# Two DRAM accumulators in turn for the routed experts' results, with no wait behind each scatter

## The chip, the cores and the metric

The kernel runs on one core of a Trainium2 chip. The metric is the device time of one execution in microseconds (us), the median of several runs. A core has a matrix engine (PE, with a separate row PEld for its weight loads), a vector engine (DVE), a scalar engine (ACT), GpSimd (POOL), a queueing engine (SP) and 16 DMA engines that all its queues share.

## What is computed

One layer of a decoder for 512 prompt tokens and 64 sample tokens (576 in all, width 1024, all float32): a mixer of pooling and two kinds of attention, then a mixture of experts. Only the last matters here:

```python
scores = jax.nn.sigmoid(jnp.einsum('nd,de->ne', xf, w_router, ...))
_, top_idx = lax.top_k(scores + router_bias.astype(jnp.float32), TOP_K)      # 8 of 64 experts
top_w = top_s / jnp.sum(top_s, axis=-1, keepdims=True) * ROUTED_SCALE
...
def one_block(args):
    xb, e = args
    return swiglu(xb, we_gate[e], we_up[e], we_down[e])                      # 1024 -> 256 -> 1024
y_rows = lax.map(one_block, (x_rows, block_exp)).reshape(n_rows, d)
return jax.ops.segment_sum(y_rows * row_w[:, None], row_tok, num_segments=n_tok + 1)[:n_tok]
...
y = routed_experts(...) + swiglu(xf, ws_gate, ws_up, ws_down)                # plus a shared expert
```

Tokens are sorted by expert into blocks of 128 rows that belong to one expert each; a block's rows are gathered, go through the expert, and are added back to their tokens. After it come an RMSNorm, a gate and the residual sum.

## The kernel before

Each engine runs a program of its own, written out by hand, and they meet in semaphores. The routed part is a loop over pairs of blocks (35 pairs with these inputs; the number is computed on the chip). In a pair, j is 0 or 1.

- **POOL** (lines 985 to 1017) gathers the rows of the next pair from the DRAM tensor `h2rows` into `xg[:, j]` (L1001), as soon as `t_done` says that PE has transposed the rows of this pair. Then it copies the pair's row numbers and weights into `scol` and `wcol` (L1006, L1007; `cols_ready`). Then, for each j, it waits until ACT and DVE have written the result `yb[:, j]`, issues a scatter that adds it to the DRAM tensor `yacc` (L1014, an indirect DMA with an add), **waits for its landing** (L1015) and counts `added`. All of POOL's DMAs are in queue q0.
- **PE** transposes the gathered rows (L2275, 8 instructions for a block), multiplies with gate and up of block 0 and of block 1 (16 records of L1836 each at 0.43 us), turns the activations (L2290) and multiplies with down. The transposes of block 1 wait for the pair before to be copied out of its bank.
- **ACT and DVE** copy the transposed rows (L1271, L1799), form the activation (L1294, L1804), copy it back turned (L1281), and write `yb` (L1288, L1809), scaled by `wcol`, after `added` says that the scatter before has read the buffer. ACT also waits for the weights and passes that on to PE as `weights_in` (L1264).
- **SP** (L845, L847, L851) fetches each expert's gate, up and down (1 MB each, queue q1) into one of two buffers. Gate and up of an expert are issued when PE has finished gate and up of the expert two before it (`gu_done`), down when the down product has (`d_done`), strictly one after another: the second block's gate and up stand behind the first block's down.

Before the loop the shared expert's results go into `yacc` (L857), which also has 128 rows for padding (L858). After it SP waits for all scatters, reads `yacc` back (L881), ACT takes the sum of squares (L1312), DVE normalises (L1817 to L1827) and SP writes the outputs.

Of the kernel before, what the change touches and what calls it, by code (L numbers as in the profile page):

```python
# [47 lines left out]
def parts(t):  # L48
    return P if t < PT_ else NS
# [258 lines left out]
def build(nc, x_prompt, x_sample, cache_b1, cache_b2, cache_b3, cache_c, state_pool, c_prompt, c_sample,  # L308
# [14 lines left out]
    with ExitStack() as ctx:  # L323
# [8 lines left out]
        def at(off, *dims):  # L332
# [4 lines left out]
            if len(dims) == 3:  # L337
# [34 lines left out]
        h2rows = nc.dram_tensor("h2rows", [TOK, D], F32, kind="Internal").ap()  # L372
        yacc = nc.dram_tensor("yacc", [TOK + P, D], F32, kind="Internal").ap()

# [104 lines left out]

        g2mod = at(8 * D, 2, D)  # L480


# [39 lines left out]
                             "at_ready", "d_done", "y_act", "y_dve"))  # L522
        added, weights_in = sem("added"), sem("weights_in")
        yacc_in, cols_ready, g2_in = sem("yacc_in"), sem("cols_ready"), sem("g2_in")
        f_in = [sem(f"f_in{t}") for t in range(TILES)]
        f_ssq, f_root, f_rn, f_out = (sem(n) for n in ("f_ssq", "f_root", "f_rn", "f_out"))

# [94 lines left out]
        def _(sp):  # L622
# [232 lines left out]
            for t in range(TILES):  # L855
                wait_emptied(sp, ("sy", t, 1))
                sp.dma_start(yacc[toks(t), :], ysh[0:parts(t), t, :]).then_inc(yacc_in, 16)  # L857
            sp.dma_start(yacc[TOK:TOK + P, :], ysh[:, 0, :]).then_inc(yacc_in, 16)  # L858

# [18 lines left out]
            for j in range(2):  # L878
                sp.wait_ge(y_out[j], 16 * n_pairs)
            for t in range(TILES):  # L880
                sp.dma_start(ysh[0:parts(t), t, :], yacc[toks(t), :]).then_inc(f_in[t], 16)  # L881
            for j in range(2):
# [13 lines left out]
        def _(pool):  # L896
# [86 lines left out]
            n_pairs = pool.value_load(pairs[0:1, 0:1], min_val=1, max_val=NBLK // 2)  # L983
            pool.sem_inc(added, 2)

            for j in range(2):
# [4 lines left out]
                                        ).then_inc(xg_in[j], 16)  # L991
            pool.wait_ge(yacc_in, 16 * (TILES + 1))
            with pool.Fori(0, n_pairs) as i:

                for j in range(2):

                    pool.wait_ge(t_done, 2 * i + j + 3)
                    pool.tensor_copy(icol[:, j:j + 1], rowtok[:, bass.ds(2 * i + j + 2, 1)]).then_inc(icol_ready, 1)  # L998
                    pool.wait_ge(icol_ready, 2 * i + j + 3)
                    pool.sem_inc(gather_ticks, 1)  # L1000
                    pool.indirect_dma_start(xg[:, j, :], None, h2rows,  # L1001
                                            bass.IndirectOffsetOnAxis(ap=icol[:, j:j + 1], axis=0)
                                            ).then_inc(xg_in[j], 16)

                for j in range(2):
                    pool.tensor_copy(scol[:, j:j + 1], addrow[:, bass.ds(2 * i + j, 1)]).then_inc(cols_ready, 1)  # L1006
                    pool.tensor_copy(wcol[:, j:j + 1], wtab[:, bass.ds(2 * i + j, 1)]).then_inc(cols_ready, 1)  # L1007
                pool.wait_ge(cols_ready, 4 * i + 4)

                for j in range(2):  # L1010
                    pool.wait_ge(y_act, 2 * i + j + 2)
                    pool.wait_ge(y_dve, 2 * i + j + 2)
                    pool.sem_inc(gather_ticks, 1)
                    pool.indirect_dma_start(yacc, bass.IndirectOffsetOnAxis(ap=scol[:, j:j + 1], axis=0),  # L1014
                                            yb[:, j, :], None, compute_op=ALU.add).then_inc(y_out[j], 16)  # L1015
                    pool.wait_ge(y_out[j], 16 * i + 16)
                    pool.sem_inc(added, 1)


        @block.scalar  # L1020
        def _(act):
# [245 lines left out]
            with act.Fori(0, n_pairs) as i:  # L1267
# [15 lines left out]
                def result(j):  # L1283

                    act.wait_ge(added, 2 * i + j + 1)
                    act.wait_ge(d_done, 2 * i + j + 3)
                    act.wait_ge(cols_ready, 4 * i + 2 * j + 2)
                    act.activation(yb[:, j, 0:512], psb[6 if j == 0 else 2][:, :], ACT.Copy,  # L1288
                                   scale=wcol[:, j:j + 1]).then_inc(y_act, 1)
# [16 lines left out]
            for t in range(TILES + 1):  # L1306
                if t < TILES:
                    r = parts(t)
                    act.wait_ge(f_in[t], 16)
                    if t:  # L1310
                        act.wait_ge(f_ssq, t)
                    act.activation(junk2[0:r, :], ysh[0:r, t, :], ACT.Square,  # L1312
                                   accum_out=stat[0:r, 3, t:t + 1]).then_inc(f_ssq, 1)
# [7 lines left out]
        def _(dve):  # L1321
# [371 lines left out]
            shared_act(1)  # L1693

            total, nblk, ends, r0 = (starts[:, n, :] for n in range(4))

# [99 lines left out]
            with dve.Fori(0, n_pairs) as i:  # L1796
# [8 lines left out]
                for j in range(2):  # L1805
                    dve.wait_ge(added, 2 * i + j + 1)
                    dve.wait_ge(d_done, 2 * i + j + 3)
# [3 lines left out]


            for t in range(TILES + 1):
                if t < TILES:
                    st = stat[0:parts(t), 3, t:t + 1]
                    dve.wait_ge(f_ssq, t + 1)
                    dve.tensor_scalar(st, st, 1.0 / D, EPS, ALU.mult, ALU.add).then_inc(f_root, 1)  # L1817
# [521 lines left out]
```

## Time and profile before

| | |
|---|---|
| median of 3 runs | 2154.64 us (2152.85 to 2161.73) |
| span of the profiled execution | 2140.2 us |
| its mean granted TensorE clock | 0.915 |
| busy in it: PE / PEld / DVE / ACT / POOL | 1869.5 / 1155.5 / 463.4 / 369.2 / 298.4 us |
| loop over pairs in it | 1098.6 to 2105.1 us |
| weights fetched by SP's queue q1 in the loop | 62 experts of 3 MB |

Times in a trace are counted from the span's start. A wait is shown as the idle time of an engine in front of an instruction, and the arrow names what ended it. The landing of a DMA is the time at which its semaphore tells of it. The clock is the share of full speed that the chip granted to TensorE.

### The profile page before, as it was taken

To read this page: it belongs to the slowest core of one execution; us is meant where nothing else is said; L and a number is where in the kernel's file an instruction comes from. 1 tells how busy PE (TensorE), PEld (TensorE's weight loads), DVE (VectorE), ACT (ScalarE), POOL (GpSimd) and SP (SyncE) were. 2 spreads that over 40 slices of the span, in tenths; PEclk is the share of its full clock that TensorE was granted. 3 is DMA by queue.
4 is the path that set the end of the run, shared out by engine and by line. 5 is a ranking of instruction groups with operands and counts; after the bars stand their busy time and mean duration, and the time that the engine had idled before them with its cause. 6 is when DMAs were issued, how large, how long until landed. Compare 5 with 4: busy or idle time off the path is not lost.

```text
span 2140.2 us, 22425 instructions
## 1 busy us (share of the span) xinstructions
PE 1869.5 (87%) x6907; PEld 1155.5 (54%) x6908; DVE 463.4 (22%) x1188; ACT 369.2 (17%) x1013; POOL 298.4 (14%) x462
## 2 busy tenths in 40 slices
PE   7899999998899999996968988899789877898873
PEld 1268887878797777544434434444344443344431
DVE  2120001464421111244621111111011111111112
ACT  2100002463320000132101111111111111111111
POOL 0110410020000000010012212222212222211221
PEclk9999999589999999998979998999899898998987
DMA  9843693505786543300058888887788788878875
GB/s 308 303 135 37 183 330 129 166 3 187 234 257 198 157 135 115 121 30 15 30 214 293 261 291 282 285 281 231 265 289 265 253 255 303 284 255 289 285 239 152
DMA packets 147723, 446.40 MB, mean 209 GB/s; under 512 B 10734, under 2 KB 76142, under 8 KB 121879
## 3 DMA queue, kind: packets, MB, share of 16 engines
q1 hardware_dynamic: 125555, 326.43, 44.0%
q0 software_dynamic: 22112, 119.21, 20.7%
q8 instruction: 37, 0.61, 0.1%
q14 instruction: 19, 0.16, 0.0%
HBM read 392.87 MB, written 97.48 MB: 229 GB/s over the span
## 4 chain that ended last, share of the span: by engine, by line
PE 60%; DMA 27%; DVE 5%; issue 4%; SPq 1%; POOL 1%; ACT 1%; POOLq 0%; DVEq 0%; ACTq 0%
PE bank L1836 55%; DMA yacc<-arena,scol 17%; DMA arena<-h2rows,icol 8%; PE bank L2275 2%; PE bank L2058 1%; PE bank L1993 1%; POOL arena L1001 1%; DMA pscale<-in_pool_scale 1%; DMA mods<-arena 1%; DVE arena L1809 1%; DMA arena<-in_w_ada 1%; SPq L639 0%; PE bank L2290 0%; PE bank L1860 0%; POOL icol L998 0%
## 5 line engine op out<-in xcount | busy, mean ns | idle before, releaser
L1836 PE MATMUL bank<-arena 128*128 (+8 forms) x5656 | 1706.2, 459 | 54.1 <-ACTq L1264 15.2
L1836 PEld LDWEIGHTS bank<-arena 128*128 128x128 f32 (+3 forms) x5656 | 987.7, 200 | 675.6 <-issue 564.6
L2275 PE MATMUL bank<-ident,arena 128*128 128x128 f32 x560 | 101.4, 339 | 147.1 <-DMA arena<-h2rows,icol 144.3
L1014 POOL DMA_INDIRECT yacc<-arena,scol x70 | 112.1, 1602 | 505.5 <-DMA yacc<-arena,scol 354.3
L2275 PEld LDWEIGHTS bank<-ident,arena 128*128 128x128 f32 x560 | 86.1, 203 | 178.0 <-DMA arena<-h2rows,icol 115.0
L1033 ACT ACTIVATE arena<-bank 128x512 f32<-128x512 f32 (+7 forms) x152 | 75.9, 505 | 378.7 <-PE bank L1836 223.2
L1804 DVE TENSOR_TENSOR arena<-bank,arena 128x256 f32<-128x256 f32 x70 | 29.7, 425 | 501.5 <-ACT arena L1294 501.5
L1809 DVE TENSOR_SCALAR arena<-bank,wcol 128x512 f32<-128x512 f32 x70 | 51.5, 749 | 223.7 <-POOL wcol L1007 113.9
L1333 DVE COPY arena<-bank 128x512 f32<-128x512 f32 (+8 forms) x74 | 43.7, 593 | 243.1 <-PE bank L1836 178.5
L1294 ACT ACTIVATE arena<-bank 128x256 f32<-128x256 f32 x70 | 26.9, 384 | 372.1 <-PE bank L1836 262.1
L1799 DVE COPY arena<-bank 128x512 f32<-128x512 f32 x70 | 48.4, 692 | 165.6 <-PE bank L2275 165.6
L1288 ACT ACTIVATE arena<-bank,wcol 128x512 f32<-128x512 f32 x70 | 48.1, 687 | 182.1 <-POOL wcol L1007 90.1
L1001 POOL DMA_INDIRECT arena<-h2rows,icol x70 | 70.9, 1013 | 59.8 <-POOL icol L998 56.6
L1271 ACT ACTIVATE arena<-bank 128x512 f32<-128x512 f32 x70 | 41.8, 597 | 176.9 <-PE bank L2275 175.9
L970 POOL DMA_DIRECT2D out<-in_cache_b x24 | 12.1, 513 | 346.4 <-PE bank L1836 280.1
L1180 ACT ACTIVATE arena<-bank 128x288 f32<-128x288 f32 x48 | 19.7, 411 | 217.1 <-PE bank L1836 217.1
L1281 ACT ACTIVATE arena<-bank 128x256 f32<-128x256 f32 x70 | 26.9, 384 | 160.7 <-PE bank L2290 160.7
L998 POOL COPY icol<-arena 128x1 uint32 x70 | 13.2, 189 | 240.9 <-DMA yacc<-arena,scol 229.2
L2290 PEld LDWEIGHTS bank<-ident,arena 128*128 128x128 f32 x140 | 27.3, 195 | 33.1 <-issue 24.7
L1618 DVE SCALAR_TENSOR_TENSOR arena<-bank,pscale,arena 128x288 f32<-128x288 f32 x16 | 8.3, 518 | 169.0 <-PE bank L1836 169.0
L978 POOL TENSOR_TENSOR arena<-arena 128x1024 f32<-128x1024 f32 (+1 forms) x5 | 11.7, 2341 | 169.7 <-DVE arena L1674 169.7
L1123 ACT ACTIVATE arena<-arena,nmx 128x128 f32<-128x128 f32 (+1 forms) x80 | 34.8, 437 | 1.2 <-DVE nmx L1504 1.2
(249 smaller groups left out, 690.8 us busy)
## 6 DMA issues: line engine op xcount, KB each, us to landing
arena<-in_we_gate SPq DMA_DIRECT2D x64, 1024.0 KB, 6.4
arena<-in_we_up SPq DMA_DIRECT2D x64, 1024.0 KB, 10.3
arena<-in_we_down SPq DMA_DIRECT2D x64, 1024.0 KB, 7.9
out<-in_cache_b POOLq DMA_DIRECT2D x8, 4080.0 KB, 16.1
arena<-in_w_ada SPq DMA_DIRECT2D x12, 2048.0 KB, 17.6
arena<-in_cache_b SPq DMA_DIRECT2D x18, 1024.0 KB, 7.6
arena<-in_w_in SPq DMA_DIRECT2D x7, 2048.0 KB, 8.2
arena<-in_w_in SPq DMA_DIRECT2D x24, 512.0 KB, 5.8
```

Of the source, the lines that this page charges most:

```text
L1001: pool.indirect_dma_start(xg[:, j, :], None, h2rows, bass.IndirectOffsetOnAxis(ap=icol[:, j:j + 1], axis=0)).then_inc(xg_in[j], 16)
L1014: pool.indirect_dma_start(yacc, bass.IndirectOffsetOnAxis(ap=scol[:, j:j + 1], axis=0), yb[:, j, :], None, compute_op=ALU.add).then_inc(y_ ...
L1033: act.activation(out, pick(bank), ACT.Copy).then_inc(emptied["A"], 1)
L1123: ins = act.activation(v, v, ACT.Exp, bias=nmx[:, s % 4, h:h + 1], accum_out=den[:, s % 4, h:h + 1])
L1271: act.activation(xT[:, j, 0:512], psb[2 * j][:, :], ACT.Copy).then_inc(xt_act, 1)
L1288: act.activation(yb[:, j, 0:512], psb[6 if j == 0 else 2][:, :], ACT.Copy, scale=wcol[:, j:j + 1]).then_inc(y_act, 1)
L1333: dve.tensor_copy(out, pick(bank)).then_inc(emptied["D"], 1)
L1799: dve.tensor_copy(xT[:, j, 512:1024], psb[2 * j + 1][:, :]).then_inc(xt_dve, 1)
L1804: dve.tensor_tensor(a, psb[4 + j][:, FF:2 * FF], e, ALU.mult).then_inc(a_ready, 1)
L1809: dve.tensor_scalar(yb[:, j, 512:1024], psb[7 if j == 0 else 3][:, :], wcol[:, j:j + 1], None, ALU.mult).then_inc(y_dve, 1)
L1836: return pe.matmul(out, lhsT, rhs, start=first, stop=last)
L2275: ins = pe.transpose(psb[2 * j + k // 4][:, P * (k % 4):P * (k % 4 + 1)], xg[:, j, k:D:KD], ident[:, :])
```

## The change

There are two accumulators, `yacc[0]` and `yacc[1]`; block j of every pair adds to `yacc[j]`. POOL no longer waits behind a scatter. The wait for the landing of the scatter of the same j moves to the next pair, in front of the copies of `scol`, whose buffer the scatter reads. ACT and DVE wait for `y_out[j]` itself, and the count `added` is gone. `yacc[1]` begins as zeros (a memset of `yb[:, 1]` on DVE, stored by SP tile by tile), the padding rows are stored by POOL, and at the end both accumulators are read and DVE sums them.

```diff
-        yacc = nc.dram_tensor("yacc", [TOK + P, D], F32, kind="Internal").ap()
+        yacc = [nc.dram_tensor(f"yacc{j}", [TOK + P, D], F32, kind="Internal").ap() for j in range(2)]
...
+        yother = at(A_W1, TILES, D)
...
-                sp.dma_start(yacc[toks(t), :], ysh[0:parts(t), t, :]).then_inc(yacc_in, 16)
-            sp.dma_start(yacc[TOK:TOK + P, :], ysh[:, 0, :]).then_inc(yacc_in, 16)
+                sp.dma_start(yacc[0][toks(t), :], ysh[0:parts(t), t, :]).then_inc(yacc_in, 16)
+                if t == 0:
+                    sp.wait_ge(zeros_ready, 1)
+                sp.dma_start(yacc[1][toks(t), :], yb[0:parts(t), 1, :]).then_inc(yacc_in, 16)
...
-                sp.wait_ge(y_out[j], 16 * n_pairs)
+                sp.wait_ge(y_out[j], 16 * n_pairs + 16)
             for t in range(TILES):
-                sp.dma_start(ysh[0:parts(t), t, :], yacc[toks(t), :]).then_inc(f_in[t], 16)
+                sp.dma_start(ysh[0:parts(t), t, :], yacc[0][toks(t), :]).then_inc(f_in[t], 16)
+                sp.dma_start(yother[0:parts(t), t, :], yacc[1][toks(t), :]).then_inc(f_in[t], 16)
...
-            pool.sem_inc(added, 2)
...
-            pool.wait_ge(yacc_in, 16 * (TILES + 1))
+            pool.wait_ge(zeros_ready, 1)
+            for j in range(2):
+                pool.dma_start(yacc[j][TOK:TOK + P, :], yb[:, 1, :]).then_inc(y_out[j], 16)
+            pool.wait_ge(yacc_in, 16 * 2 * TILES)
...
                 for j in range(2):
+
+                    pool.wait_ge(y_out[j], 16 * i + 16)
                     pool.tensor_copy(scol[:, j:j + 1], addrow[:, bass.ds(2 * i + j, 1)]).then_inc(cols_ready, 1)
...
-                    pool.indirect_dma_start(yacc, bass.IndirectOffsetOnAxis(ap=scol[:, j:j + 1], axis=0),
+                    pool.indirect_dma_start(yacc[j], bass.IndirectOffsetOnAxis(ap=scol[:, j:j + 1], axis=0),
                                             yb[:, j, :], None, compute_op=ALU.add).then_inc(y_out[j], 16)
-                    pool.wait_ge(y_out[j], 16 * i + 16)
-                    pool.sem_inc(added, 1)
...
-                    act.wait_ge(added, 2 * i + j + 1)
+                    act.wait_ge(y_out[j], 16 * i + 16)
...
-                    act.wait_ge(f_in[t], 16)
+                    act.wait_ge(f_sum, t + 1)
...
+            dve.wait_ge(h2_out, 16 * PT_)
+            dve.memset(yb[:, 1, :], 0.0).then_inc(zeros_ready, 1)
...
-                    dve.wait_ge(added, 2 * i + j + 1)
+                    dve.wait_ge(y_out[j], 16 * i + 16)
...
+            def both(t):
+
+                r = parts(t)
+                dve.wait_ge(f_in[t], 32)
+                dve.tensor_tensor(ysh[0:r, t, :], ysh[0:r, t, :], yother[0:r, t, :], ALU.add).then_inc(f_sum, 1)
+
+            both(0)
             for t in range(TILES + 1):
+                if t + 1 < TILES:
+                    both(t + 1)
```

POOL's loop over pairs before, in the order in which it is issued. The two scatters are L1014; the second waits for `y_out0`, the landing of the first, and the loop's end waits for `y_out1`.

```order
104 L998 ISA [waits t_done]
105 L998 COPY icol<-arena 128x1
106 L1001 DMA arena<-h2rows,icol 128x1024 [waits icol_ready]
...
120 L1011 REGISTER_ALU [waits cols_ready]
121 L1014 DMA yacc<-arena,scol 704x1024 [waits y_act,y_dve]
122 L1016 ISA
123 L1014 DMA yacc<-arena,scol 704x1024 [waits y_out0,y_act,y_dve]
124 L993 REGISTER_ALU [waits y_out1]
125 L993 COMPARE_AND_BRANCH
```

The same loop after the change.

```order
106 L1004 ISA [waits t_done]
107 L1004 COPY icol<-arena 128x1
108 L1007 DMA arena<-h2rows,icol 128x1024 [waits icol_ready]
...
114 L1014 ISA [waits y_out0]
115 L1014 COPY scol<-arena 128x1
...
118 L1014 ISA [waits y_out1]
119 L1014 COPY scol<-arena 128x1
...
124 L1022 DMA yacc<-arena,scol 704x1024 [waits y_act,y_dve] x2
125 L999 REGISTER_ALU
```

The waits for landings have moved from behind each scatter to a place behind the next pair's gathers, so neither the second scatter nor the gathers stand behind a landing.

DVE's tail before: from the first tile's statistics to the end of its sum with the residual and on to the second tile's statistics.

```order
791 L1817 TENSOR_SCALAR stat<-stat 128x1 [waits f_ssq] x2
792 L1823 RECIPROCAL stat<-stat 128x1 [waits f_rn]
793 L1826 SCALAR_TENSOR_TENSOR arena<-arena,stat 128x1024 [waits g2_in,dve_step]
794 L1827 TENSOR_TENSOR arena<-arena 128x1024 [waits dve_step]
795 L1817 TENSOR_SCALAR stat<-stat 128x1 [waits f_ssq]
```

The same place after the change, where L1826 is the sum of the two accumulators.

```order
793 L1826 TENSOR_TENSOR arena<-arena 128x1024 [waits f_in0]
794 L1826 TENSOR_TENSOR arena<-arena 128x1024 [waits f_in1]
795 L1835 TENSOR_SCALAR stat<-stat 128x1 [waits f_ssq]
796 L1826 TENSOR_TENSOR arena<-arena 128x1024 [waits f_in2]
797 L1835 TENSOR_SCALAR stat<-stat 128x1 [waits f_ssq]
798 L1841 RECIPROCAL stat<-stat 128x1 [waits f_rn]
799 L1844 SCALAR_TENSOR_TENSOR arena<-arena,stat 128x1024 [waits g2_in,dve_step]
800 L1845 TENSOR_TENSOR arena<-arena 128x1024 [waits dve_step]
```

A sum of 1024 columns stands in front of each tile's work, one tile ahead.

## Rows read from the trace of the kernel before

**Rows 1.** The page, part 4: the chain that ended last, by line.

```profile
PE bank L1836 55%; DMA yacc<-arena,scol 17%; DMA arena<-h2rows,icol 8%; PE bank L2275 2%; PE bank L2058 1%; PE bank L1993 1%; POOL arena L1001 1%; DMA pscale<-in_pool_scale 1%; DMA mods<-arena 1%; DVE arena L1809 1%; DMA arena<-in_w_ada 1%; SPq L639 0%; PE bank L2290 0%; PE bank L1860 0%; POOL icol L998 0%
```

**Rows 2.** Waits in the loop (1130 to 2110): total us, times, longest us.

```profile
POOL yacc L1014 <- DMA yacc<-arena,scol: 354.3, 34, 12.3
...
POOL icol L998 <- DMA yacc<-arena,scol: 229.2, 34, 10.4
...
PE bank L2275 <- DMA arena<-h2rows,icol: 129.5, 34, 8.4
...
DVE arena L1809 <- POOL wcol L1007: 113.9, 16, 9.2
...
PE bank L1836 <- ACTq L1264: 15.2, 12, 2.4
```

**Rows 3.** Timeline of POOL: start, us, instruction, [idle time before it and what ended it].

```profile
1549.84 1.62 POOL L1014 DMA_INDIRECT yacc<-arena,scol  x1 [7.65 <-DVE arena L1809]
1561.96 1.57 POOL L1014 DMA_INDIRECT yacc<-arena,scol  x1 [10.51 <-DMA yacc<-arena,scol]
1572.37 0.18 POOL L998 COPY icol<-arena 128x1 uint32 x1 [8.84 <-DMA yacc<-arena,scol]
1573.39 1.03 POOL L1001 DMA_INDIRECT arena<-h2rows,icol  x1 [0.83 <-POOL icol L998]
```

**Rows 4.** Timeline of PE over the same pairs and the next two.

```profile
1553.53 7.03 PE L1836 MATMUL bank<-arena 128*128 x16
1561.56 3.70 PE L1836 MATMUL bank<-arena 128*128 x8 [1.00 <-ACTq L1264]
...
1581.58 1.97 PE L2275 MATMUL bank<-ident,arena 128*128 128x128 f32 x8 [5.57 <-DMA arena<-h2rows,icol]
...
1609.91 1.05 PE L2275 MATMUL bank<-ident,arena 128*128 128x128 f32 x8
...
1633.15 1.04 PE L2275 MATMUL bank<-ident,arena 128*128 128x128 f32 x8
```

**Rows 5.** Timeline of SP's queue: down of one block, gate of the next.

```profile
1548.10 0.33 SPq L851 DMA_DIRECT2D arena<-in_we_down  x1
1550.19 0.33 SPq L845 DMA_DIRECT2D arena<-in_we_gate  x1
```

**Rows 6.** Stretches: engines' busy us (instructions), granted clock, DMA share, GB/s.

```profile
1098.60:2105.10 1006.50, 855.83 (x2372) 423.85 (x2372) 129.14 (x210) 143.68 (x280) 213.48 (x349) 0.92 0.83 269
1549.00:1566.00 17.00, 15.83 (x50) 7.90 (x49) 2.56 (x5) 2.65 (x5) 3.19 (x2) 1.00 1.00 349
1900.00:2000.00 100.00, 80.36 (x226) 40.63 (x225) 13.10 (x21) 14.20 (x27) 18.90 (x31) 0.88 0.88 293
```

**Rows 7.** DMA queues, 1106 to 2106: packets, MB, share of 16 engines' time.

```profile
q1 hardware_dynamic: 26826, 195.26, 52.3%
q0 software_dynamic: 19837, 72.22, 30.2%
```

**Rows 8.** DMA queues, 1555 to 1561, one scatter beside weights.

```profile
q1 hardware_dynamic: 204, 1.42, 59.2%
q0 software_dynamic: 144, 0.52, 44.0%
```

**Rows 9.** Before the loop: DVE's timeline, and SP's queue q1 from 1010 to 1084.

```profile
1013.18 0.22 DVE L1698 COPY arena<-bank 128x64 f32<-128x64 f32 x1 [8.11 <-PE bank L1836]
...
q1 hardware_dynamic: 800, 2.88, 10.8%
```

**Rows 10.** Timeline of the tail, POOL, SP, ACT and DVE.

```profile
2109.42 1.58 POOL L1014 DMA_INDIRECT yacc<-arena,scol  x1 [5.33 <-DMA yacc<-arena,scol]
2115.78 2.29 SPq L881 DMA_DIRECT2D arena<-yacc  x5
2119.39 1.06 ACT L1312 ACTIVATE arena<-arena 128x1024 f32<-128x1024 f32 x1 [14.39 <-DMA arena<-yacc]
...
2135.63 1.22 DVE L1827 TENSOR_TENSOR arena<-arena 64x1024 f32<-64x1024 f32 x1
```

More of the change, by code:

```diff
@@ L522, in build @@
                              "at_ready", "d_done", "y_act", "y_dve"))
-        added, weights_in = sem("added"), sem("weights_in")
+        weights_in, zeros_ready = sem("weights_in"), sem("zeros_ready")
         yacc_in, cols_ready, g2_in = sem("yacc_in"), sem("cols_ready"), sem("g2_in")
         f_in = [sem(f"f_in{t}") for t in range(TILES)]
-        f_ssq, f_root, f_rn, f_out = (sem(n) for n in ("f_ssq", "f_root", "f_rn", "f_out"))
+        f_sum, f_ssq, f_root, f_rn, f_out = (sem(n) for n in ("f_sum", "f_ssq", "f_root", "f_rn", "f_out"))
         def wait_fill(eng, key):
```

## The prediction, made before the changed kernel was run

> **What bounds the kernel now.** I read the chain first, then the waits of the loop, then timelines of single pairs. In the chain [rows 1] PE's matmuls hold 55%, and behind them stand two transfers: scatters 17%, gathers 8%. The loop over 35 pairs takes 1006.5 of the 2140.2 us [rows 6], 28.76 us a pair, and this is where the change acts. Its waits [rows 2] show one chain from end to end: POOL's second scatter waits for the first to land (354.3 us, 34 times), POOL's next gather waits for the second (229.2 us), PE's transposes wait for that gather (129.5 us), and DVE's results wait for the weights column that POOL copies late (113.9 us, 16 times). One pass through it: first scatter 1549.84, second 1561.96, next pair's gather 1573.39 [rows 3], transposes 1581.58, after 5.57 us of idle [rows 4]. Nothing but POOL's order made that gather late, since its buffer was free once PE had done the transposes before gate and up at 1553.53 [rows 4].
>
> What the pair costs without that chain shows in one pair that waited for nothing: from transposes 1609.91 to transposes 1633.15 [rows 4], **23.24 us**. So 35 x (28.76 - 23.24) = 193 us of the loop are idle time or slow clock. The stalls also cost clock: the transposes after a stall take 1.97 us for 8, the unstalled ones 1.05 and 1.04 [rows 4], which is 1.2 against 2.4 GHz; the loop's mean clock is 0.92 [rows 6]. The Trainium skill, "TensorE: Matmul & The Clock Gate", part 1, says that a gate passes half of the clock's pulses when the engine has been idle; the trace agrees, by the 1.97 and 1.04 us.
>
> **The change, part by part.**
>
> *The wait behind each scatter goes.* POOL's program for a pair then is: gathers, wait for both scatters of the pair before, four small copies, two scatters. The gathers can be issued as soon as the transposes are done, some 20 us ahead of their use instead of 8 us. PE's 129.5 us of waits for gathers and DVE's 113.9 us for the column should nearly vanish, and with them the clock's falls. If nothing took their place, the loop would be 35 x 23.24 = 813 us, 193 less.
>
> *What is late next: the DMA engines.* In 1000 us of the loop the weights' queue q1 takes 52.3% and POOL's queue q0 30.2% of the engines' time [rows 7]: 523 and 302 us. 1000 us hold 34.8 pairs, so q0 costs 302 / 34.8 = 8.7 us a pair (two gathers, two scatters). The loop fetches 62 experts, 523 / 62 = 8.44 us each, 16.9 us in a pair that fetches two. Together **25.6 us of DMA time for a full pair**, more than PE's 23.24. By SP's issues 28 pairs fetch two experts, 6 fetch one, the last none; those 7 are left to PE (8.44 + 8.7 is under 23.24). The stretch 1549 to 1566 has a DMA share of 1.00 while PE is busy 15.83 of 17 us [rows 6], so a full DMA is possible, but only while enough is queued. SP does not queue ahead: the second block's gate and up are issued 2.09 us after the first block's down (1548.10, 1550.19) [rows 5], and PE wants them at 1553.53 + 7.03 = 1560.56. It got them at 1561.56, with one scatter beside them: 1.00 us late [rows 4]. Over the loop such waits were 15.2 us, the longest 2.4 [rows 2]. This 1.00 us I add to every full pair, since all of them will now run on this tight schedule: 26.6 us.
>
> Sum of the loop: 28 x 26.6 + 7 x 23.24 = 744.8 + 162.7 = 907.5 us, **99.0 us less** than 1006.5.
>
> Bounds of this term: at the low end transfers fit in, and a full pair costs PE's time and the 1.00 us seen: 28 x 24.24 + 162.7 = 841.4, 165 less. At the high end DMA reaches only the share of a dense 100 us of before, 0.88 [rows 6]: 25.6 / 0.88 = 29.1, 28 x 29.1 + 162.7 = 977.5, 29 less. I take the value between, nearer to the trace's 1.00 over 17 us than to 0.88, because that 0.88 has POOL's own order in it, which emptied q0 for 8 us at a time.
>
> *Waits that move.* The copies of the columns now wait for both landings. One scatter by itself kept POOL waiting 12.3 us at the longest [rows 2], 14 with its issue. Its first 5 us bring no data: all 0.52 MB of the one issued at 1549.84 [rows 3] moved between 1555 and 1561 [rows 8]. Two in a row share that start, so with q0's 8.7 us doubled by sharing both are in after at most 5 + 17 = 22 us; as the gathers behind them are in the 8.7 too, and a scatter took 6 us of its time, more likely 5 + 12 = 17. They are issued just before and just after the transposes, and the column is wanted 23.24 less two result steps of some 2 us, that is 19 us after them. That is thin; it mostly costs nothing, and a late pair pays 1 or 2 us, which the high end holds. ACT's and DVE's waits on y_out ask for the same landing as the column does, so they add nothing.
>
> *Before the loop.* DVE's memset stands in front of a wait of 8.11 us for PE [rows 9]; even at 1.22 us, the price of 1024 columns in a sum [rows 10], it is hidden. Without that cover it would cost 1.22. SP's five extra stores lie in a stretch where q1 is busy 10.8% of 74 us, 8.0 us for 2.88 MB [rows 9]; hidden too. POOL's two padding stores, 1.05 MB or 2.9 us at that rate, now lie behind the first gathers, beside the first weights; one such store was in SP's queue before. Bounds 0 and 2.9; I take **1.5 us**, half, since only part of the first weights is awaited.
>
> *After the loop.* The second scatter is issued after the last result instead of at 2109.42 [rows 10], about 3.5 us earlier, but the DMA time of the first is in its way: 3 us gained. Then twice the bytes are read back. The first tile came 3.6 us after SP's issue at 2115.78 [rows 10]; its partner adds 1.3 us, and one sum of 1.22 us [rows 10] precedes its square. After that DVE is the bound, with five sums more, 6.1 us in all. The first one's wait and four further sums, less what DVE idled between tiles: 7 us. Bounds 5 and 9. Net **4 us** lost.
>
> Sum: -99.0 + 1.5 + 4 = -93.5. The profiled span becomes 2140.2 - 93.5 = 2046.7. The runs' median lies 14.4 us above that span (launch and end lie outside it), and I shift it alike: 2154.6 - 93.5 = **2061 us**.
>
> **The rivals.**
>
> *A. The weights' wait takes the gather's place, and the clock falls again: slower.* Place: PE in front of the second block's gate and up. From 1555 to 1561 one scatter took 44.0% and the weights 59.2% of the engines' time [rows 8], so each us in which q0 is busy there costs the weights 0.4 us. Before, the scatter's data began to move only near 1555, so the weights had 1550 to 1555 alone. If the first scatter moves earlier, at 2.5 us, and the second and a gather follow without a gap, weights are beside q0 for the whole of 1552 to 1564 and finish 3 us later still: a wait of 4 us. If such a wait halves the clock, as the 5.57 us idle did, gate and up of a block (7.03 us) take up to twice as long, say 3.5 us more. A full pair is then 23.24 + 4 + 3.5 = 30.7, the loop 28 x 30.7 + 162.7 = 1022, the time 2154.6 + 16 + 5.5 = **2176**. It decides at (1006.5 - 162.7) / 28 = 30.1 us a full pair. Against it: the 12 waits of that kind seen were 1.3 us on average [rows 2] and PE's clock stayed at 1.00 in that stretch [rows 6]. The Trainium skill, "DMA: Bandwidth & Descriptors", section "Queues, rings and completion order", says that a DMA engine goes round the queues that have work, packet by packet, so a full q0 always takes its turns from the weights; the trace agrees with 44.0 against 59.2%. By this rule alone, with no order between the transfers, this rival is what the change invites.
>
> *B. The gathers are late again, in q0.* They now stand behind two scatters in one queue. If q0's 8.7 us are doubled by sharing (17.4) plus 5 us of start, the second gather lands some 22 us after the transposes, wanted after 24 to 25. For it: little room. If it came 2 us late in every full pair, with DMA empty meanwhile, the pair is 28.6 and the loop 963.5, 43 less: **2117**.
>
> *C. All fits.* Low end of the loop: 2154.6 - 165 + 5.5 = **1995**. For it: weights can come 1.00 us late and no later. Against: 25.6 us of DMA do not fit in 24.24, unless packets got slow only by contention.
>
> *D. The change doesn't do what it says:* POOL would still wait for landings, now in front of the columns, and results wait for the columns. If that cost what it did before (113.9 us, twice as often since now in every pair), 228 us against the 243 that go: about **2145**. Against: the landings have a whole pair's time.
>
> **How the numbers follow.** Forecast 2035 to 2090: 0.55. C and what lies towards it, under 2035: 0.20. B and poor DMA use, 2090 to 2144: 0.13. D, within 0.5% (10.8 us, about what a measurement of this kernel tells from no change): 0.05. A: 0.07. The range leaves out A, D, the worst of B and the best of C: 2005 to 2125. Faster 0.88, same 0.05, slower 0.07.
>
> **What the profile after would show.** Right, if POOL's waits for scatters shrink to a few us, gathers are issued within 3 us of the transposes, the time between the unawaited transposes is 25.5 to 27.5 us in full pairs, the DMA share in the loop rises from 0.83 to 0.91, the clock to about 1.0, and the wait of L1836 for L1264 grows from 15.2 us to 60 or 90. Wrong, if PE's waits for weights exceed 3 us a pair and the clock stays at 0.92 (A), if transposes still wait for gathers (B), or if DVE's results wait for the column in most pairs (D). The tail should read: last result to end 39 us instead of 35.

## The result, and the profile after

| | before | after |
|---|---|---|
| median of 4 runs | 2154.80 us (2152.85 to 2161.73) | 2013.76 us (2002.48 to 2022.74) |
| ratio to before | | 0.9339, 95% interval 0.9302 to 0.9376 |
| span of the profiled execution | 2140.2 us | 2010.7 us |
| loop over pairs in it | 1006.5 us | 872.6 us |
| last result to the end | 35.1 us | 40.4 us |
| mean granted clock in it | 0.915 | 0.946 |

The changed kernel is 141 us faster. The range held it, the size did not: 2061 us had been forecast. The span shrank by 129.5 us: the loop gave 133.9, the part before it 0.9, and the tail cost 5.3. The medians moved 11.5 us further than the spans. The profiled execution of after was itself timed, at 2012.53 us, so only 1.8 us lie around its span; with the same 1.8 us the profiled execution of before took some 2142 us, a quick one beside its median of 2154.8. The prediction had put all of its 14.4 us around the span.

After, the page's part 4, the chain that ended last, by line, which answers to [rows 1] (L1854 is the helper that was L1836, L1022 the scatter, L1007 the gather):

```profile
PE bank L1854 66%; DMA arena<-in_we_up 14%; PE bank L2076 1%; PE bank L2011 1%; PE bank L2293 1%; DMA pscale<-in_pool_scale 1%; PE bank L2308 1%; DMA arena<-h2rows,icol 1%; DMA arena<-in_w_ada 1%; DMA mods<-arena 1%; SPq L871 1%; SPq L870 1%; SPq L846 1%; SPq L640 0%; DMA yacc<-arena,scol 0%
```

Scatters have gone from 17% to nothing and gathers from 8 to 1%. In their place stands a transfer that was not in the chain before: the weights of the up product, 14%. The waits in the loop (1130 to 1975) answer to [rows 2]:

```profile
POOL yacc L1022 <- DVE arena L1818: 352.3, 66, 13.2
POOL scol L1014 <- DMA yacc<-arena,scol: 217.2, 62, 4.8
DVE arena L1818 <- PE bank L1854: 192.6, 68, 3.0
...
PE bank L1854 <- ACTq L1270: 42.5, 25, 5.1
```

POOL now waits for results, as it should. It still waits 217.2 us for landings, in front of the columns, but nobody stands behind it: DVE's results (L1818) wait for PE alone, and no wait for gathers is left in this stretch. PE's wait for weights, passed on by ACT at L1270, has grown from 15.2 us in 12 times to 42.5 in 25.

One full pair on PE after, beside [rows 4], and the loop and a stretch of it beside [rows 6]:

```profile
1745.14 1.05 PE L2293 MATMUL bank<-ident,arena 128*128 128x128 f32 x8
...
1747.33 7.03 PE L1854 MATMUL bank<-arena 128*128 x16
1755.14 3.70 PE L1854 MATMUL bank<-arena 128*128 x8 [0.78 <-ACTq L1270]
...
1769.43 1.05 PE L2293 MATMUL bank<-ident,arena 128*128 128x128 f32 x8
```

```profile
1097.70:1970.30 872.60, 820.85 (x2372) 400.74 (x2372) 129.80 (x210) 143.53 (x280) 216.22 (x349) 0.99 0.91 311
...
1300.00:1400.00 100.00, 95.16 (x279) 46.46 (x278) 15.51 (x25) 17.01 (x33) 26.40 (x42) 1.00 0.97 327
```

The pair takes 24.29 us, the 23.24 of an unstalled one and 1.05 more, mostly the 0.78 us for weights. It is one of the shorter ones: of the 25 waits for weights half are over 1.33 us. The clock is at 0.99 instead of 0.92 in the loop, and the same 2372 instructions keep PE busy for 820.85 instead of 855.83 us: of the 134 us gained, 35 are the faster clock in PE's own work. The DMA share rose from 0.83 to 0.91. The queues from 1106 to 1960, beside [rows 7]:

```profile
q1 hardware_dynamic: 26886, 195.75, 59.6%
q0 software_dynamic: 19895, 72.41, 32.5%
```

In the tail SP reads both accumulators once both scatters have landed, and ACT's first square waits for DVE's sum, beside [rows 10]:

```profile
1980.20 0.33 SPq L884 DMA_DIRECT2D arena<-yacc  x1
...
1986.25 1.06 ACT L1318 ACTIVATE arena<-arena 128x1024 f32<-128x1024 f32 x1 [16.00 <-DVE arena L1826]
```

### The profile page after: what moved, and what is told of

Same layout as the page of the kernel before. It is cut to its first block, busy times and chain, and to the rows that moved or that the text cites. A ratio compares the mean times of both kernels' runs of the same rounds, so it can differ in the third digit from the quotient of the medians.

```text
span 2010.7 us, 22441 instructions
## 1 busy us (share of the span) xinstructions
PE 1832.8 (91%) x6907; PEld 1131.9 (56%) x6908; DVE 470.2 (23%) x1194; ACT 368.4 (18%) x1013; POOL 302.3 (15%) x464
## 4 chain that ended last, share of the span: by engine, by line
PE 71%; DMA 18%; DVE 4%; SPq 4%; issue 2%; ACT 1%; POOL 0%; ACTq 0%; POOLq 0%; DVEq 0%
PE bank L1854 66%; DMA arena<-in_we_up 14%; PE bank L2076 1%; PE bank L2011 1%; PE bank L2293 1%; DMA pscale<-in_pool_scale 1%; PE bank L2308 1%; DMA arena<-h2rows,icol 1%; DMA arena<-in_w_ada 1%; DMA mods<-arena 1%; SPq L871 1%; SPq L870 1%; SPq L846 1%; SPq L640 0%; DMA yacc<-arena,scol 0%
## 5 line engine op out<-in xcount | busy, mean ns | idle before, releaser
L1854 PE MATMUL bank<-arena 128*128 (+8 forms) x5656 | 1695.0, 457 | 82.6 <-ACTq L1270 42.5
L1854 PEld LDWEIGHTS bank<-arena 128*128 128x128 f32 (+3 forms) x5656 | 979.6, 198 | 699.8 <-issue 586.4
L1022 POOL DMA_INDIRECT yacc<-arena,scol x70 | 112.1, 1602 | 373.7 <-DVE arena L1818 368.7
L1818 DVE TENSOR_SCALAR arena<-bank,wcol 128x512 f32<-128x512 f32 x70 | 52.6, 751 | 198.3 <-PE bank L1854 198.3
L2293 PE MATMUL bank<-ident,arena 128*128 128x128 f32 x560 | 78.0, 283 | 21.0 <-DMA arena<-h2rows,icol 15.4
L2293 PEld LDWEIGHTS bank<-ident,arena 128*128 128x128 f32 x560 | 71.5, 193 | 43.5 <-issue 19.5
L1007 POOL DMA_INDIRECT arena<-h2rows,icol x70 | 70.7, 1010 | 60.2 <-POOL icol L1004 56.7
L1014 POOL COPY scol<-arena 128x1 uint32 x70 | 12.9, 184 | 220.2 <-DMA yacc<-arena,scol 217.2
L2308 PEld LDWEIGHTS bank<-ident,arena 128*128 128x128 f32 x140 | 27.4, 195 | 33.1 <-issue 24.7
```

The lines of the kernel that those rows point to most:

```text
L1007: pool.indirect_dma_start(xg[:, j, :], None, h2rows, bass.IndirectOffsetOnAxis(ap=icol[:, j:j + 1], axis=0)).then_inc(xg_in[j], 16)
L1022: pool.indirect_dma_start(yacc[j], bass.IndirectOffsetOnAxis(ap=scol[:, j:j + 1], axis=0), yb[:, j, :], None, compute_op=ALU.add).then_inc ...
L1818: dve.tensor_scalar(yb[:, j, 512:1024], psb[7 if j == 0 else 3][:, :], wcol[:, j:j + 1], None, ALU.mult).then_inc(y_dve, 1)
L1854: return pe.matmul(out, lhsT, rhs, start=first, stop=last)
L2293: ins = pe.transpose(psb[2 * j + k // 4][:, P * (k % 4):P * (k % 4 + 1)], xg[:, j, k:D:KD], ident[:, :])
L2308: ins = pe.transpose(psb[j][:, k * P:(k + 1) * P], act3[:, 3 * j + 2, k:FF:2], ident[:, :])
```

## The experiments

Each kernel ran in turns with the kernel before on the same chip. Ratios are to the kernel before; pairs are timed from ACT's copy of one pair's second block to that of the next, and numbered from 0. A full pair is one in which SP fetches two experts. A trace is of one run of its kernel, which can lie up to 18 us from the median (e4's does), so loop lengths that differ by a few us are not told apart.

### Which of the two waits matters

e1 puts both waits back behind the scatters, in the kernel with two accumulators:

```diff
                     pool.indirect_dma_start(yacc[j], ...).then_inc(y_out[j], 16)
+                    pool.wait_ge(y_out[j], 16 * i + 32)
```

> The changed kernel with the wait for the landing put back behind each scatter; the two accumulators, the stores ahead of the loop and the sums behind it stay. If the gain is all in POOL's order (my theory), the loop is back at some 1000 us and the whole at 2155 to 2165, the time before plus some 5 us of tail. If the second accumulator itself helped (the rival: two adds to one tensor slow each other in memory), it stays under 2120.

Measured: 2161.9 us, ratio 1.002 (0.9987 to 1.0052). The time is in the range of its theory. The loop is back at 1024 us, and the three waits of [rows 2] are back too:

```profile
POOL yacc L1022 <- DMA yacc<-arena,scol: 273.0, 26, 12.5
...
POOL icol L1004 <- DMA yacc<-arena,scol: 195.5, 28, 10.4
...
PE bank L2294 <- DMA arena<-h2rows,icol: 119.3, 28, 8.4
```

(waits of e1, 1130 to 1960, a shorter stretch than in [rows 2]). The second accumulator by itself gives nothing. All of the gain is POOL's order, which the second accumulator allows: with it the two scatters of a pair never add to the same tensor.

e2 puts a wait behind the first scatter only, e3 behind the second only:

```diff
+                    if j == 0:                # e3: j == 1
+                        pool.wait_ge(y_out[j], 16 * i + 32)
```

> The changed kernel with a wait for the landing behind the first scatter only: the second scatter, and the gathers behind it, start some 8 us later than in the changed kernel, but no gather waits for the second landing. Theory: most of the gain comes from freeing the gathers of the second landing, since gathers issued 11 to 13 us after the transposes still have about 12 us; 2015 to 2050. Rival: the two scatters must overlap for any gain, over 2080.

> The changed kernel with a wait for the landing behind the second scatter only: the scatters overlap, but the next gathers are issued only when the second has landed, some 15 us after the transposes instead of 3. Theory: gathers then land about when PE wants them or a few us later, 2040 to 2100. Rival: the place of the wait does not matter, only that there is one less, and e2 and e3 give the same time within 10 us.

Measured: e2 2038.1 us, ratio 0.944 (0.9375 to 0.9504), loop 892 us; e3 2079.5 us, ratio 0.9645 (0.958 to 0.971), loop 932 us. Both fell in their theories' ranges. Taking away the second wait alone (e2) brings some 119 of the 141 us; taking away the first alone (e3) some 77. They sum to more than the whole: either one removed shortens the same chain. But e3's range was met for another reason than the one given. Its gathers, issued some 17 us after the transposes begin (4.5 us in the changed kernel), land 5.3 us later in the median, and PE waits only 9.1 us for them in all. What it loses shows in the weights, which are later, and with them in the clock (72 us of the loop at half speed, against 20 in the changed kernel). Why later gathers go with later weights is not shown:

```profile
POOL icol L1004 <- DMA yacc<-arena,scol: 357.7, 31, 13.3
...
PE bank L1856 <- ACTq L1272: 63.5, 23, 5.4
...
PE bank L2295 <- DMA arena<-h2rows,icol: 9.1, 6, 2.5
```

(waits of e3, 1130 to 1960).

### One accumulator with the changed order

If the second accumulator gives nothing, one should do, as in e2: the second scatter waits for the landing of the first, since both may add to the same row (what would be lost without that wait was not run), and the next gathers follow its issue. The padding rows are stored in two halves, so that both landing counts start as in the changed kernel.

```diff
-                    pool.indirect_dma_start(yacc[j], ...).then_inc(y_out[j], 16)
+                    pool.indirect_dma_start(yacc, ...).then_inc(y_out[j], 16)
+                    if j == 0:
+                        pool.wait_ge(y_out[j], 16 * i + 32)
...
-                dve.tensor_tensor(ysh[0:r, t, :], ysh[0:r, t, :], yother[0:r, t, :], ALU.add).then_inc(f_sum, 1)
```

> One accumulator as before, but with the changed order: the second scatter waits for the landing of the first, and the next gathers are issued behind it with no wait for its own landing (that comes in front of the next columns). No second tensor, no sums at the end. By e2 the loop takes some 892 us; the tail is 5 us shorter than with two accumulators: 2028 to 2040. If two adds to one tensor cost the loop anything by themselves it is over 2045.

Measured: 2025.8 us, ratio 0.9366 (0.9326 to 0.9406), the loop 893.0 us and the tail 35.1. That is 2 us under its range of 2028 to 2040, and not over the 2045 of the other theory. The loop is 20 us longer than with two accumulators, as in e2 (892), and the tail 5.3 shorter. By the intervals it can't be told from the changed kernel. Two adds to one tensor cost nothing of their own here when the second waits for the first; two in flight at once on one tensor were not run.

### Does a longer wait for weights bring the clock down?

e5 holds every second expert's gate and up back, to test rival A:

```diff
-                    sp.wait_ge(gu_done, done)
+                    sp.wait_ge(t_done if j == 1 else gu_done, done + 2 if j == 1 else done)
```

> The changed kernel with the gate and up fetch of every second expert held back until PE has transposed the block two after the expert's last: some 2.5 us later than in the changed kernel in a pair whose second block it belongs to, more in the others. It tests rival A, that a longer wait for weights lets the clock fall and costs far more than itself. If waits of 3 to 4 us leave the clock up, a full pair costs 26 to 27.5 us, the whole 2060 to 2110, and the mean clock stays above 0.93. If the clock falls as after the 5.57 us stalls of before, a pair costs 29 us or more, the whole is over 2140 and the half-speed time in the loop is over 100 us (20 in the changed kernel).

Measured: 2335.9 us, ratio 1.0829 (1.0788 to 1.087). This is the side on which the clock falls (over 2140 us, over 100 us at half speed), but far beyond it, because I had the delay wrong. SP's loop runs over experts and PE's over blocks. An expert with two blocks shifts one against the other, and in the shifted pairs PE stands still for about 12 us and not 2.5: these pairs take 35 to 39 us. PE in such a pair:

```profile
1309.16 1.12 PE L2293 MATMUL bank<-ident,arena 128*128 128x128 f32 x8 [0.16 <-ACT arena L1294]
1322.58 12.78 PE L1854 MATMUL bank<-arena 128*128 x24 [12.29 <-issue]
```

Without a stall 24 such records take 10.46 us (e4 and e10, below), so 2.3 us were lost to the clock after the wait; 341 us of the loop were at half speed, most of them while PE stood still. In the pairs that were not shifted (1 and 2) the fetch was held some 2.5 us, and they took 29.3 and 30.3 us instead of 24.8 and 24.6:

```profile
1138.59 5.39 PE L1854 MATMUL bank<-arena 128*128 x8 [4.13 <-ACTq L1270]
...
1167.83 6.49 PE L1854 MATMUL bank<-arena 128*128 x8 [4.05 <-ACTq L1270]
```

So rival A's mechanism exists: a wait of 4 us, as the prediction priced it, and then 1.7 and 2.8 us of clock (8 such records take 3.70 us at full clock), where the prediction had 3.5. Held by 2.5 us, a pair pays about twice the delay; where PE stood for 12 us it paid 13 to 14, little more than the wait itself.

### SP's order

PE's wait for weights, 0.68 us and more a pair, could be SP's lateness or the DMA engines' limit. e4 issues gate and up of both experts of a pass first, then down of both:

```diff
+                both_of = []
...
-                    expert_weights(j, bass.ds(expert, 1), done)
+                    both_of.append((j, bass.ds(expert, 1), done))
+                for args in both_of:
+                    gate_up_weights(*args)
+                for args in both_of:
+                    down_weights(*args)
```

> The changed kernel with SP's order changed: gate and up of both blocks of a pair first, then down of both, so that the second block's gate and up are issued when PE has finished with them, some 3 to 5 us earlier, instead of behind the first block's down. Theory 1 (the wait of about 1 us a pair is SP's order): the wait goes, the loop falls from 873 towards 35 x 23.24 = 813 plus some us, the whole to 1965 to 1985. Theory 2 (the DMA engines are full, 24.3 us of transfers in a pair): the DMA time is the floor, and the whole stays at 2000 to 2015.

Measured: 2046.7 us, ratio 0.9478 (0.9409 to 0.9546), **slower** than the changed kernel, which neither theory had. Pair by pair it falls in two groups. Pairs 1, 2, 19 and 20, in which a pass of SP matches a pair of PE, take 23.2 us with two fetches; here pair 2, 1148.86 to 1172.10:

```profile
1148.86 1.05 PE L2302 MATMUL bank<-ident,arena 128*128 128x128 f32 x8
...
1172.10 1.05 PE L2302 MATMUL bank<-ident,arena 128*128 128x128 f32 x8
```

The shifted pairs take 24 to 30 us, since a block's down now stands behind gate and up of a block that PE finishes half a pair later. A new wait shows there, for down (waits of e4, 1130 to 1960; it was 17.0 us in 7 times in the changed kernel, 1130 to 1975):

```profile
ACT arena L1296 <- DMA arena<-in_we_down: 73.5, 15, 5.7
```

e6 keeps the order and only loads the registers of both experts of a pass ahead:

```diff
+                both_of = []
                 for j in range(2):
                     expert = sp.value_load(...)
                     done = sp.value_load(...)
-                    expert_weights(j, bass.ds(expert, 1), done)
+                    both_of.append((j, bass.ds(expert, 1), done))
+                for args in both_of:
+                    expert_weights(*args)
```

> The changed kernel, in which SP loads the registers of both experts of its loop pass (their numbers and waits) ahead of the first fetch, so that the second's gate and up follow the first's down at once instead of 2.1 us later; the order and the waits are unchanged. If SP's lateness is what PE's wait of about 1 us a pair consists of (theory 1, after e4's pairs of 23.2 us with two fetches), most of these waits go: a loop of 835 to 850 us, the whole 1975 to 1992. If the DMA engines are the floor, nothing moves: 2005 to 2020.

Measured: 2078.3 us, ratio 0.9624 (0.9597 to 0.9652), again slower, and again for the shift. In matching pairs gate follows down after 0.5 us, and they take 23.9 to 24.4 us (24.6 to 25.1 in the changed kernel). In shifted pairs the boundary of SP's pass, now with four register loads, lies between down and gate:

```profile
1217.41 0.33 SPq L852 DMA_DIRECT2D arena<-in_we_down  x1
1220.77 0.34 SPq L846 DMA_DIRECT2D arena<-in_we_gate  x1
```

The gap is 3.36 us instead of 2.09 [rows 5], and PE pays:

```profile
1222.83 7.03 PE L1857 MATMUL bank<-arena 128*128 x16
1233.18 6.69 PE L1857 MATMUL bank<-arena 128*128 x8 [3.32 <-ACTq L1273]
```

A wait of 3.32 us, and then 6.69 us for 8 records that take 3.70 at full clock. **A gap 1.3 us longer made these pairs some 4 us longer** (28.6 us in the median where the changed kernel has 24.8): about 2.5 us of wait and 3 of clock in the pair shown, against 0.8 us of wait. The expectation was missed, but the run shows that a longer gap makes the wait longer. Whether a shorter one takes all of it away it leaves open: in the matching pairs 0.42 to 0.90 us stayed.

e8 therefore turns SP's loop round by one step, so that the next expert's registers are loaded before the wait for the down product, whatever the shift:

```diff
                 for j in range(2):
+                    e, done = fetch_of(2 * i + (j + 2))
+                    following, then = fetch_of(2 * i + (j + 3))
+                    down_weights(j, e, done)
+                    gate_up_weights(1 - j, following, then)
```

> The changed kernel with SP's loop turned round by one step: it loads the registers of the next expert before it waits for the down product, so gate and up follow the down ahead of them at once, in pairs of either alignment. In the kernel where the registers of two experts were loaded together, pairs whose gap grew from 2.1 to 3.4 us took 4 us longer and those whose gap shrank 0.5 us less. If that gap is the cause of the waits for weights, nearly every full pair takes 23.2 to 23.9 us, the loop 820 to 840, the whole 1958 to 1980. If the DMA engines are the floor (24.3 us), it stays over 2000.

Measured: 1991.9 us, ratio 0.9257 (0.9229 to 0.9284), better than the changed kernel. The gap is 0.53 us in all pairs and the bad pairs are gone (waits for weights 23.7 us in 25 times, 1.6 at most). But full pairs take 24.2 to 24.5 us (one 24.8; 23.2 only the four behind a pair with one fetch), not 23.2 to 23.9, and the total lies between the ranges of both theories. The usual wait has stayed. The down product's fetch and PE's start on the second block behind it, first in the changed kernel, then in e8:

```profile
1766.19 0.33 SPq L852 DMA_DIRECT2D arena<-in_we_down  x1
1779.32 3.69 PE L1854 MATMUL bank<-arena 128*128 x8 [0.68 <-ACTq L1270]
```

```profile
1724.58 0.33 SPq L855 DMA_DIRECT2D arena<-in_we_down  x1
1737.68 3.70 PE L1873 MATMUL bank<-arena 128*128 x8 [0.80 <-ACTq L1289]
```

It is 13.1 us in both, though e8's gate was issued 0.53 us behind the down and the other 2.08 (1768.27). Over all pairs the changed kernel's waits for weights run from 0.68 to 5.11 us, half of them over 1.33, and e8's from 0.75 to 1.57, half of them over 0.93. So a long gap at SP makes waits longer, but some 0.8 us is left even with the shortest. What is left is the order, down ahead of gate and up, and the time that the 3 MB then take.

> The kernel with one accumulator, the second scatter behind the landing of the first and the gathers behind its issue, with SP's loop turned round. Its tail is 5 us shorter than with two accumulators, but its second scatter and gathers go some 8 us later. If the weights' lateness was what separated its loop (893 us) from the two accumulators' (873), both come to the same loop and it is 5 us faster: 1953 to 1975. If the late gathers cost it by themselves, its loop stays 15 us or more longer: 1975 to 1995.

Measured: e9 2020.2 us, ratio 0.9398 (0.9369 to 0.9426). The loop is 880.0 us against e8's 848.1: with SP's long gaps gone, one accumulator's later scatters and gathers do cost, some 32 us in the loop for 6 in the tail. Not by gathers that PE waits for (0.8 us, 1130 to 1930), but again by the weights: PE's wait for them is 43.3 us in 24 times. So two accumulators are worth 1.4% here, once the weights are in time. The second theory held in direction; the time lay 25 us over its range.

Last, e10 shifts e4's passes by one expert, so that they match PE's pairs where e4's did not:

```diff
...
+            e, done = fetch_of(2)
+            gate_up_weights(0, e, done)
+            down_weights(0, e, done)
+            with sp.Fori(0, more - 1) as i:
+                e, done = fetch_of(2 * i + 3)
+                following, then = fetch_of(2 * i + 4)
+                gate_up_weights(1, e, done)
+                gate_up_weights(0, following, then)
+                down_weights(1, e, done)
+                down_weights(0, following, then)
...
```

> As e4 (gate and up of two experts first, then down of both), but with the two experts of a pass of SP's loop shifted by one, so that a pass matches PE's pair where e4's did not. In e4 pairs 1, 2, 19 and 20, which fetch two experts and match, took 23.2 us and the 23 others with two fetches 25 to 30. If SP's order in relation to PE's pair is the cause, it is now the other way round: pairs 5 to 10, 14 to 17 and 24 to 33 take 23.2 to 23.6 us, pairs 1, 2, 19 and 20 about 27.5, the loop 830 to 850, the whole 1970 to 1990. If the DMA engines need 24.3 us for two fetches over many pairs in a row, and e4's pairs were only single ones that drew on a pause before, the matching pairs stay at 24.2 us or more and the whole at 1995 or more.

Measured: **1978.7 us**, ratio 0.9198 (0.9153 to 0.9243), the loop 835.8 us. Pairs 5 to 10, 14 to 17 and 24 to 33 all take 23.2 us, and pairs 1 and 2 went from 23.2 in e4 to 29.1 and 28.4 (19 and 20, to 24.9 and 25.9). Two stretches of such pairs, and the queues from 1690 to 1780:

```profile
1690.00:1780.00 90.00, 89.35 (x266) 44.44 (x265) 14.49 (x24) 16.40 (x32) 24.81 (x40) 1.00 1.02 365
1200.00:1350.00 150.00, 148.86 (x447) 74.41 (x446) 25.10 (x40) 27.55 (x53) 41.12 (x64) 1.00 1.02 359
```

```profile
q1 hardware_dynamic: 3454, 25.17, 68.9%
q0 software_dynamic: 2106, 7.67, 33.3%
```

PE is busy 89.35 of 90 us, with a DMA share of 1.02 beside it. (A share is the sum of the packets' times, so it can come out a little over 1.) So the DMA engines are full but not in the way: all transfers of a full pair fit in 23.24 us. This kernel beats the others with these inputs. Its order suits the shift that these inputs happen to have; e8's serves both.

## Why the prediction was right in kind and too small

- **What bounds the kernel.** Right. The chain through both landings to the gather was the loop's stall, as e1 shows by putting it back, and nothing in the changed kernel waits for a gather or a column.
- **The loop, -99.0 us forecast, -133.9 measured.** Here the sum failed, in the term of 26.6 us for a full pair. With 7 pairs at 23.24, 872.6 us leave 25.4 for each of the 28 full ones; 18 of them took 24.2 to 25.2, and a few with longer waits for weights 26 to 31. Two steps made the term too large. First, 25.6 us of DMA time a full pair: in the stretch of e10 above 90 us hold 3.87 full pairs at 68.9 + 33.3%, which is 23.8 us a pair. By the same reckoning the changed kernel's own records give 24.4 us. The records of before charge 8% more than e10's for the same transfers, why is not shown: a packet's time there is no measure of the least it can take. Second, I added the 1.00 us of wait to that floor, as if a full DMA and a late weight were two costs. But the last 0.8 us of the wait seems to be how full DMA engines show on PE when the down product's weights go first: the queues take 72.4 + 30.7% from 1744 to 1755, before the wait shown above, e8's shorter gap did not take it away, and another order, with the same transfers, did (e10). The wait belongs on PE's own 23.24, and there 1.00 us was too small: the 25 waits are 1.7 us on average, and some are followed by slow clock. So the low bound, 28 x (23.24 + 1.00), gives a loop of 841.4 us, 31 too short, as the forecast's 907.5 is 35 too long. A floor that does not bind and a wait taken too short partly cancelled; that the range held the result owes something to this.
- **The low bound was held unlikely for a wrong reason.** "25.6 us of DMA do not fit in 24.24" was the argument against rival C. The transfers fit in 23.24 (e10). The prediction had named the way out itself, "unless packets got slow only by contention", and gave it too little weight. Rival C's 1995 us, the value for full pairs of 24.24 us, was reached by e8 (1991.9), whose pairs are at 24.4, and not by the changed kernel.
- **Waits that move.** Right: POOL waits 217.2 us for landings in front of the columns, at no cost.
- **Before the loop, +1.5 forecast.** It was -0.9; the first transposes wait for the first gather, which the padding stores stand behind, not before.
- **After the loop, +4 forecast.** +5.3, inside its bounds. From the last result to the read it is 9.9 us instead of 10.7, so 0.8 us were gained and not 3; from there to the end 30.5 instead of 24.4, so 6.1 were lost and not 7. The two errors partly cancel. DVE's sums are what the rest waits on, as forecast.
- **Rival A.** It did not decide the result, but it is real (e5, e6). Even the changed kernel has pairs of this kind: one of 31.0 us, in which weights issued at 1660.87 let PE wait until 1676.34.

```profile
1664.20 7.03 PE L1854 MATMUL bank<-arena 128*128 x16
1676.34 6.05 PE L1854 MATMUL bank<-arena 128*128 x8 [5.11 <-ACTq L1270]
```

Why these transfers took so much longer than their neighbours is open.
- **Rivals B and D.** B did not occur: a gather takes 14.5 us in the median from issue to landing, up from 6.7, and is still in time. D did not occur: POOL does wait for landings in front of the columns, but in no pair from 1130 to 1975 does a result wait for a column.
- **The signs named.** The clock (0.99) and the DMA share (0.91) came as named. POOL's waits for scatters did not shrink to a few us: they are 217.2 us, moved to where they cost nothing. The gathers are issued 4.5 us after the transposes begin, not within 3, and the tail is 40.4 us, not 39. The wait for weights (42.5 us) stayed below the 60 to 90. Most full pairs were below the 25.5 to 27.5.
- **The median.** Of the 47 us between forecast and result, 35 are the loop's term, 2.4 the start's and -1.3 the tail's; the other 11 are the gap between the profiled execution of before and its median.

## What to carry to other kernels

A wait for a DMA's landing in a queue's program delays whatever is issued behind it, so look first for what stands there without needing the landing; here moving the second wait behind the next gathers brought most of the gain with no second accumulator (e7). Once a stall is gone, the next limit may be the order in which another queue issues: two loops that count different things (experts and blocks) drift against each other, and an order that is free in one position can cost in the other (23.2 against 24 to 30 us a pair in e4). A DMA share near 1 need not be a bound: take the least time of a transfer from a stretch where the engines are kept full, and don't add a wait that comes from that same limit.

## What the runs showed of the hardware that I had not expected

- The clock falls to its lower level after rather short waits: one of 3.32 us (e6) made 8 records take 6.69 us instead of 3.70, while e8's waits, none over 1.57 us, left it at 1.00. So 1.3 us of delay in SP's queue cost some 4 us a pair. But the length of the wait alone does not decide it. In the changed kernel 3.65 us left the next 8 records at full clock, and 2.13 us did not:

```profile
1283.52 3.69 PE L1854 MATMUL bank<-arena 128*128 x8 [3.65 <-ACTq L1270]
...
1704.33 5.39 PE L1854 MATMUL bank<-arena 128*128 x8 [2.13 <-ACTq L1270]
```

- How two queues share the engines depends on what they carry. After, the queues from 1750 to 1758, in which q0 carries scatters, and then from 1761 to 1766, in which it carries gathers:

```profile
q1 hardware_dynamic: 223, 1.70, 52.5%
q0 software_dynamic: 215, 0.82, 51.1%
```

```profile
q1 hardware_dynamic: 193, 1.45, 68.5%
q0 software_dynamic: 191, 0.71, 34.6%
```

In both stretches the two queues get nearly the same number of packets (223 and 215, 193 and 191), though the weights' are twice as large and though a scatter's packet takes longer than a gather's. That is what the Trainium skill, "DMA: Bandwidth & Descriptors", section "Queues, rings and completion order", states (engines go round the queues packet by packet), and the equal counts fit it more plainly than the shares of time did.
